# A fused decoder layer on one Trainium2 core: expert weights in 4 MB halves, the block tables moved behind block 9, the residual added on TensorE

## The chip, the cores and the metric

The kernel runs on one core of a Trainium2 chip. The metric is the device time of one execution in microseconds (us). TensorE is PE in the profile (its weight loads are PEld), VectorE is DVE, ScalarE is ACT, GpSimd is POOL, SyncE is SP; a q behind an engine's name is its sequencer. All data is float32.

## The reference

One layer on 256 tokens of width 1024: a projection, a gated delta network and a dilated attention, an output projection, and a mixture of experts. Only the last is touched here:

```python
h = x + concat(a, b) @ W_out
logits = rmsnorm(h) @ w_router + b_router            # 32 experts
top_v, top_e = top_k(logits, 4); gates = softmax(top_v)
for each expert e and its tokens x:
    gu = x @ w_gu[e] + b_gu[e]                       # 1024 -> 2048
    g, u = min(gu[:, :1024], 7), clip(gu[:, 1024:], -7, 7)
    y = ((u + 1) * g * sigmoid(1.702 * g)) @ w_dn[e] + b_dn[e]
    out[token] += gate * y
return h + out
```

## The kernel before

The first fifth of the time is the layer up to the router. The mixture then runs as blocks of at most 64 slots of one expert. Blocks 0 to 31 are experts 0 to 31 in order; further blocks exist only where an expert has over 64 tokens, and with this input there are exactly 32. Each block reads 12 MB of weights: gate and up as four tiles of 2 MB (two of eight row groups k each), down as two of 2 MB. Gate and up have two sets of buffers in SBUF, down has one.

PE, for one block (`gate_up`, L1550, then `combine`, L1519, and `rest`, L1582): four matmuls of the bias (L1560); for each k four matmuls over 512 columns (L1569, two records each); `combine`, which adds the former block's result, scaled by the gates, to PSUM banks 0 to 3 (L1523); two transposes of the gates (L1586); the gather of the next block's tokens (L1317); the transposes of the activation (L1593), which wait for the chain of four DVE operations L1105, L1106, L1109, L1115; the transposes of the gathered rows (L1509); and the down matmuls (L1606). A wait in PE's order holds all that is behind it. The semaphores `wgu_used` (one count per tile of gate/up) and `wdn_used` (per tile of down) tell SP that a buffer is free.

SP issues the loads in an order written out by hand (`load_block(m, ahead)`, L414): the four tiles of gate/up of block m + 1 and the two of down of block m, each behind the wait for its buffer. For blocks 1 to 6 down comes last, for 7 to 9 it moves forward, from 10 on it comes first. Before the first of these loads SP waits for the table of experts (`tab_ready`, L407) and loads it into registers.

The tables (which expert a block has, each token's slot in it, its gate) are made at the start of block 0, in pieces between the k: `block_table` (L1529) after k = 0, `slot_tables` (L1536) after k = 3, and `open_mixture` (L1269), which puts the gated b_down into banks 0 to 3, after k = 5. DVE makes the counts and limits (L1047 to L1087), ACT copies the transposes (L720, L660). After the last block `combine` runs once more, DVE adds the residual in four steps (L1126) and SP writes four pieces out (L445).

## Time and profile before

| | us |
|---|---|
| median of 3 runs (1151.19 to 1152.13) | 1151.99 |
| the profiled execution | 1153.8 |
| its span, first to last instruction | 1152.0 |
| PE busy in the span | 1106.2 (96%) |
| DVE, ACT, POOL busy | 276.8, 153.8, 8.0 |
| matmuls L1569 (gate/up), 2048 records | 453.8 |
| matmuls L1606 (down), 1024 records | 226.8 |
| HBM read, over the span | 424.29 MB, 371 GB/s |
| share of the last chain: DMA, PE | 51%, 45% |

A PE that is busy for 96% need not be at its peak: matmuls are pipelined, and a record lasts longer (595 ns) than the distance to the next. The time of a stretch of PE is therefore read from the start of one group to the start of the next. A block's length is the distance between two L1560.

### The profile page before, as it was taken

What the parts mean: (1) busy time and instruction counts of PE and PEld (TensorE: products, weight loads), DVE (VectorE), ACT (ScalarE), POOL (GpSimd) and SP (SyncE); (2) the same over time, 40 slices, a digit from 0 to 9 for tenths busy, and PEclk for the clock granted to TensorE, in tenths of its full rate; (3) what the DMA queues carried; (4) which work ended last, traced back from release to release, by engine and by line L of the source; (5) the groups of instructions that cost most, each with busy time, mean ns of one, the idle gap of its engine ahead of it and who ended that gap; (6) DMA issues with size and microseconds to landing.
All of it is one profiled execution on the core that took longest, in us unless ns stands there. A gap on an engine that the chain in (4) does not pass through costs nothing.

```text
span 1152.0 us, 13668 instructions
## 1 busy us (share of the span) xinstructions
PE 1106.2 (96%) x5240; PEld 445.3 (39%) x5240; DVE 276.8 (24%) x624; ACT 153.8 (13%) x284; POOL 8.0 (1%) x28
## 2 busy tenths in 40 slices
PE   9999989999999999999999999999999999999997
PEld 7855755533333333333333333333333333333332
DVE  3642344331111111111111111111111111111112
ACT  3521314410000000000000000000000000000000
POOL 1000000000000000000000000000000000000000
PEclk9999998999999999999999999999999999999999
DMA  9594110989999999999999999999999999999995
GB/s 326 99 351 160 73 74 10 374 352 389 427 428 428 428 429 428 428 388 431 430 428 428 428 428 429 428 428 429 428 429 429 428 430 429 428 428 428 428 428 240
DMA packets 42648, 427.20 MB, mean 371 GB/s; under 512 B 6755, under 2 KB 8900, under 8 KB 18052
## 3 DMA queue, kind: packets, MB, share of 16 engines
q1 hardware_dynamic: 40340, 426.86, 89.1%
q10 hardware_dynamic: 2288, 0.07, 0.1%
q8 instruction: 13, 0.21, 0.1%
q14 instruction: 7, 0.06, 0.0%
HBM read 424.29 MB, written 2.62 MB: 371 GB/s over the span
## 4 chain that ended last, share of the span: by engine, by line
DMA 51%; PE 45%; DVE 2%; ACT 1%; issue 1%; SPq 1%; DVEq 0%; ACTq 0%
DMA store<-in_w_gate_up_dram 50%; PE bank L1569 14%; PE bank L1606 7%; PE bank L1194 5%; PE bank L1201 4%; PE bank L1393 4%; PE bank L1265 3%; PE bank L1317 2%; PE bank L1523 2%; PE bank L1560 1%; DMA store<-in_w_in_dram 1%; PE bank L1509 1%; ACT conv L731 1%; PE bank L1586 0%; PE bank L1297 0%
## 5 line engine op out<-in xcount | busy, mean ns | idle before, releaser
L1569 PE MATMUL bank<-store,conv 128*64 128x512 f32 x2048 | 453.8, 595 | 21.1 <-DMA store<-in_w_gate_up_dram 21.0
L1569 PEld LDWEIGHTS bank<-store,conv 128*64 128x64 f32 x2048 | 141.2, 137 | 329.9 <-issue 280.5
L1606 PE MATMUL bank<-store,conv 128*64 128x512 f32 x1024 | 226.8, 595 | 0.3 <-DVE conv L1118 0.3
L1105 DVE TENSOR_SCALAR conv<-bank 128x512 f32<-128x512 f32 x32 | 22.1, 691 | 661.9 <-PE bank L1569 661.9
L1606 PEld LDWEIGHTS bank<-store,conv 128*64 128x64 f32 x1024 | 70.6, 137 | 132.4 <-issue 128.0
L727 ACT ACTIVATE conv<-conv 128x512 f32<-128x512 f32 x32 | 20.1, 630 | 505.8 <-DVE conv L1105 505.8
L1523 PE MATMUL bank<-qkT 64*128 64x512 f32 x256 | 63.6, 615 | 0.7 <-ACT qkT L733 0.7
L1317 PE MATMUL bank<-arena,qkT 128*64 128x512 f32 x264 | 64.2, 605 | 0.0
L1194 PE MATMUL bank<-store 128*128 128x512 f32 x128 | 58.1, 607 | 0.0
L733 ACT COPY qkT<-bank 128x512 f32<-128x512 f32 x32 | 18.7, 585 | 252.9 <-PE bank L1606 252.9
L1201 PE MATMUL bank<-store 128*128 128x256 f32 x192 | 42.7, 380 | 0.9 <-DMA store<-in_w_in_dram 0.9
L1201 PEld LDWEIGHTS bank<-store 128*128 128x128 f32 x192 | 36.2, 190 | 7.2 <-issue 2.5
L1523 PEld LDWEIGHTS bank<-qkT 64*128 64x128 f32 x256 | 22.0, 186 | 41.8 <-issue 40.2
L1194 PEld LDWEIGHTS bank<-store 128*128 128x128 f32 x128 | 24.3, 195 | 27.5 <-issue 27.4
L1560 PE MATMUL bank<-store,qkT 32*64 32x512 f32 x256 | 34.8, 613 | 0.0
L1115 DVE TENSOR_TENSOR conv<-conv 128x512 f32<-128x512 f32 x32 | 34.4, 1076 | 0.0
L1118 DVE COPY conv<-bank 128x512 f32<-128x512 f32 x32 | 22.1, 691 | 50.5 <-PE bank L1593 50.5
L1265 PE MATMUL bank<-store,conv 128*128 128x512 f32 x64 | 30.8, 626 | 0.4 <-DVE conv L1032 0.4
L1393 PE MATMUL bank<-store 128*128 128x128 f32 x200 | 27.0, 290 | 1.9 <-DVE arena L957 1.6
L1509 PE MATMUL bank<-ident,conv 128*128 128x128 f32 x132 | 24.6, 309 | 3.5 <-ACT conv L718 0.4
L1393 PEld LDWEIGHTS bank<-store 128*128 128x128 f32 x200 | 25.5, 203 | 5.1 <-issue 2.4
L1317 PEld LDWEIGHTS bank<-arena,qkT 128*64 128x64 f32 x264 | 15.9, 136 | 24.0 <-issue 24.0
(282 smaller groups left out, 567.5 us busy)
## 6 DMA issues: line engine op xcount, KB each, us to landing
store<-in_w_gate_up_dram SPq DMA_DIRECT2D x128, 2048.0 KB, 26.8
store<-in_w_down_dram SPq DMA_DIRECT2D x64, 2048.0 KB, 19.4
store<-in_w_in_dram SPq DMA_DIRECT2D x7, 2048.0 KB, 23.1
store<-in_w_out_dram SPq DMA_DIRECT2D x1, 4096.0 KB, 18.0
bias_by_distance<-store SPq DMA_DIRECT2D x1, 1536.0 KB
hx<-in_x_dram SPq DMA_DIRECT2D x2, 512.0 KB, 3.9
store<-bias_by_distance SPq DMA_DIRECT2D x1, 1024.0 KB, 8.2
out_dram<-hx SPq DMA_DIRECT2D x4, 256.0 KB, 2.2
```

What stands on the lines that cost most here:

```text
L1105: dve.tensor_scalar(gt, bank[4][:], LIMIT, None, ALU.min).then_inc(g_min, 1)
L1115: dve.tensor_tensor(gt.rearrange("q (c r) -> q r c", c=4), up.rearrange("q (r c) -> q r c", c=4), sg.rearrange("q (r c) -> q r c", c=4), A ...
L1194: ins = mm(dst[:], xnT[:, k, half * P:(half + 1) * P], w[:, k, :], start=k == 0, stop=k == KT - 1)
L1201: ins = mm(dst[:, c * S:(c + 1) * S], w[:, k, c0:c0 + P], xnT[:, k, :], start=k == 0, stop=k == KT - 1)
L1265: last = mm(bank[H_BANK[i]][:], lhsT[:, t * P:(t + 1) * P], wout[:, k, hf * 512:(hf + 1) * 512], start=k == HG, stop=k == HG - 1)
L1317: ins = mm(bank[6][SLOTS * hf:SLOTS * (hf + 1), :], SEL[:, t, :], hn[:, t, hf * 512:(hf + 1) * 512], start=t == 0, stop=t == T - 1)
L1393: last = mm(dst[:, c], lhsT(h) if callable(lhsT) else lhsT[:, c], rhs(h) if callable(rhs) else rhs[:, c], start=start, stop=stop)
L1509: last = tp(bank[6][:, c * P:(c + 1) * P], xg_rows[:, c], ident[:])
L1523: last = mm(bank[2 * t + hf][:], SGT[SLOTS * hf:SLOTS * (hf + 1), t * P:(t + 1) * P], yb[SLOTS * hf:SLOTS * (hf + 1), :], start=False, sto ...
L1560: mm(dst[SLOTS * hf:SLOTS * (hf + 1), :], oh_cur[N_EXP * c:N_EXP * (c + 1), :], bgu[N_EXP * c:N_EXP * (c + 1), :], start=True, stop=False)
L1569: last = mm(dst[SLOTS * hf:SLOTS * (hf + 1), :], xgT[:, c:c + SLOTS], store[:, slot_at(k, odd) + c0:slot_at(k, odd) + c0 + 512], start=Fal ...
L1606: last = mm(bank[7][SLOTS * hf:SLOTS * (hf + 1), :], actT[:, c:c + SLOTS], w[:, hf * 512:(hf + 1) * 512], start=f == 0, stop=f == KT - 1)
```

## The change

- Expert numbers of blocks 1 to 28 are the loop's own count. SP no longer waits for a table before the loads; it does so before the load of block 30's gate/up (`tab_ready` 4).
- Gate/up of blocks 2 to 9 and of the last block come in tiles of 2 MB as before; those of blocks 10 to 30 come as two halves of 4 MB, whose rows in HBM are 32 KB in one piece for each partition (the tiles have 16 KB). SP waits until both tiles of a half are used, and PE waits for the whole half, before k = 0 and k = 4.
- Down of block m is issued behind gate/up of block m + 1 up to m = 15, between the halves at 16, and ahead of them from 17 on.
- Blocks 0 to 9 read slot numbers and gates directly from what the router leaves. The counts, tables and b_down stand in one piece (`late_tables`, `add_mixture`) on PE between blocks 9 and 10. There the residual is added too, as four matmuls with the identity. DVE and ACT do their part after their own block 9; PE waits for `tab_ready` 7 and then reads two registers. The rest of DVE's list of table operations is unchanged but for one more, and its copies are of 16 columns in place of 48.
- In blocks 10 to 30 `combine` stands after k = 3, in the middle of gate/up. In the last block it stands after k = 5 with the transposes of the gates, and the gather for a next block is left out.
- The out pieces are copied from PSUM, two by DVE (written out by SP) and two by ACT (which issues their DMAs itself).
- The two loads of b_down (64 KB each) stand behind those of b_gate_up on SP. The matmuls of the counts and one transpose leave PE's part ahead of block 0.

```diff
-EARLY_BLOCKS = 6
+FINE_BLOCKS = 10
+LATE_BLOCKS = 16
...
+            src = w_gate_up[0][e_ap, half * 4 * P:(half + 1) * 4 * P, :]
+            return src.rearrange("a (p i) n -> p (a i n)", p=P)
...
-            sp.wait_ge(tab_ready, 3)
...
+            def load_block(m, e, e_next, down_at, whole, off=0):
+                odd = sp.value_load(parity[0:1, bass.ds(m + (off + 1), 1)], min_val=0, max_val=1)
+                for half in range(2):
+                    if half == down_at:
+                        load_down(m, e, off)
+                    if whole:
+                        sp.wait_ge(wgu_used, 4 * m + (4 * off + 2 * half - 2))
+                        sp.wait_ge(ld_tile[2 * half], 16 * m + (16 * off + 16))
+                        sp.dma_start(half_dst(half, odd), expert_half(bass.ds(e_next, 1), half)
+                                     ).then_inc(ld_tile[2 * half], 16)
+                        continue
+                    for i in (2 * half, 2 * half + 1):
+                        sp.wait_ge(wgu_used, 4 * m + (4 * off + i - 3))
+                        if i % 2 == 0:
+                            sp.wait_ge(ld_tile[i], 16 * m + (16 * off + 16))
                         sp.dma_start(tile_dst(i, odd), expert_tile(bass.ds(e_next, 1), i)).then_inc(ld_tile[i], 16)
+                if down_at == 2:
+                    load_down(m, e, off)
...
-            with sp.Fori(1, EARLY_BLOCKS + 1) as b:
-                load_block(b, 4)
-            for k in (3, 2, 1):
-                load_block(EARLY_BLOCKS + 4 - k, k)
-            with sp.Fori(EARLY_BLOCKS + 4, n_blocks - 1) as b:
-                load_block(b, 0)
...
+            with sp.Fori(1, FINE_BLOCKS - 1) as b:
+                load_block(b, b, b + 1, 2, False)
+            with sp.Fori(FINE_BLOCKS - 1, LATE_BLOCKS) as b:
+                load_block(b, b, b + 1, 2, True)
+            with sp.Fori(LATE_BLOCKS, LATE_BLOCKS + 1) as b:
+                load_block(b, b, b + 1, 1, True)
+            with sp.Fori(LATE_BLOCKS + 1, N_EXP - 3) as b:
+                load_block(b, b, b + 1, 0, True)
...
+            load_block(three_less, expert_of(three_less + 1), e_last, 0, False, off=1)
...
+                act.wait_ge(acc_done, 2 * t + 2)
+                act.copy(hx[:, t, 512:D], bank[2 * t + 1][:]).then_inc(out_right, 1)
+                act.wait_ge(out_right, t + 1)
+                act.dma_start(out[0, t * P:(t + 1) * P, 512:D], hx[:, t, 512:D]).then_inc(st_right, 16)
...
+            for t in range(T):
+                dve.wait_ge(acc_done, 2 * t + 1)
+                dve.tensor_copy(hx[:, t, 0:512], bank[2 * t][:]).then_inc(out_left, 1)
...
+            def add_mixture(t):
                 pe.wait_ge(gT_ready, t + 1)
                 for hf in range(2):
-                    rows = slice(N_EXP * hf, N_EXP * (hf + 1))
-                    mm(bank[2 * t + hf][:], gT[t][rows, :], bdn[rows, :], start=True, stop=False,
+                    rows = slice(2 * N_EXP + N_EXP * hf, 3 * N_EXP + N_EXP * hf)
+                    mm(bank[2 * t + hf][:], gT[t][rows, :], bdn[rows, :], start=False, stop=False,
                        skip_group_check=True)
+                    mm(bank[2 * t + hf][:], ident[:], hx[:, t, 512 * hf:512 * (hf + 1)], start=False, stop=False,
...
+            def late_tables():
+                for i in range(T):
+                    ins = mm(bank[4][0:N_EXP, 0:1], mask[i], ones[:, 0:1], start=i == 0, stop=i == T - 1)
+                Tally(pe, cnt_psum).mark(ins)
+                pe.wait_ge(gates_ready, T)
+                for t in range(T):
+                    ins = tp(bank[5][:, t * P:(t + 1) * P], gates4[t], ident[:])
+                Tally(pe, gT_psum).mark(ins)
+                for t in range(T):
+                    ins = tp(bank[5][0:N_EXP, S + t * P:S + (t + 1) * P], rm[t], ident[:])
+                Tally(pe, rt_psum).mark(ins)
+                pe.wait_ge(nb_ready, 1)
+                mm(bank[4][0:N_EXP, 1:2], ucum[0:N_EXP, 0:N_EXP], more, start=True, stop=True)
+                mm(bank[4][0:N_EXP, 2:3], ustr[0:N_EXP, 0:N_EXP], more, start=True, stop=True)
+                Tally(pe, end_psum).mark(mm(bank[4][0:1, 4:5], ones[0:N_EXP, 0:1], more, start=True, stop=True))
+                for t in range(T):
+                    add_mixture(t)
...
+                pe.wait_ge(tab_ready, 3)
...
+                pe.wait_ge(tab_ready, 7)
...
+                    if k % 4 == 0:
                         pe.wait_ge(ld_tile[k // 2], 16 * (b + 1))
+                    elif k % 4 == 2 and not whole:
+                        pe.wait_ge(ld_tile[k // 2], 16 * (FINE_BLOCKS + 1) if last else 16 * (b + 1))
...
+                    if k == (5 if last else 3) and (whole or last):
+                        pe.wait_ge(y_ready, b)
+                        combine()
+                        if last:
+                            turn_gates(b)
...
+                if not last:
+                    turn_gates(b)
+                    pe.wait_ge(S_ready, b + T + 1)
+                    gather(0)
+                    gather(1).then_inc(xg_psum, 1)
...
+            def whole_block(b, odd):
+                gate_up(b, odd, whole=True)
+                rest(b)
+            def last_block(b, odd):
+                gate_up(b, odd, last=True)
+                rest(b, last=True)
...
+            expert_block(1, 1)
+            with pe.Fori(1, FINE_BLOCKS // 2) as pair:
+                expert_block(2 * pair, 0)
+                expert_block(2 * pair + 1, 1)
+            late_tables()
...
-            with pe.Fori(0, (two_less + 1) >> 1) as pair:
-                expert_block(2 * pair + 1, 1)
-                expert_block(2 * pair + 2, 0)
+            with pe.Fori(FINE_BLOCKS // 2, (two_less + 1) >> 1) as pair:
+                whole_block(2 * pair, 0)
+                whole_block(2 * pair + 1, 1)
             with pe.If((two_less + 1) & 1):
-                expert_block(two_less + 1, 1)
+                whole_block(two_less, 0)
+                last_block(two_less + 1, 1)
+            with pe.Else():
+                last_block(two_less + 1, 0)
```

## Rows read from the trace of the kernel before

**Rows 1.** The page: granted clock and GB/s in 40 slices of 28.8 us

```profile
PEclk9999998999999999999999999999999999999999
GB/s 326 99 351 160 73 74 10 374 352 389 427 428 428 428 429 428 428 388 431 430 428 428 428 428 429 428 428 429 428 429 429 428 430 429 428 428 428 428 428 240
```

**Rows 2.** The chain that ended last, in time: start us, us, what

```profile
193.16 3.44 PE bank L1265 x8
...
264.28 1.02 PE bank L1560 x8
265.30 13.88 PE bank L1569 x64
279.18 1.92 PE bank L1523 x8
...
284.77 7.02 PE bank L1606 x32
291.79 1.02 PE bank L1560 x8
...
542.65 28.06 DMA store<-in_w_gate_up_dram
```

**Rows 3.** Timeline of the SP queue, DMA issues: start us, us, line, what

```profile
238.83 14.29 SPq L428 DMA_DIRECT2D store<-in_w_gate_up_dram  x4
261.04 4.22 SPq L423 DMA_DIRECT2D store<-in_w_down_dram  x2
...
701.26 3.79 SPq L423 DMA_DIRECT2D store<-in_w_down_dram  x2
...
730.59 3.78 SPq L423 DMA_DIRECT2D store<-in_w_down_dram  x2
```

**Rows 4.** Windows: us, PE, PEld, DVE, ACT, POOL busy (x count), PEclk, DMA share, GB/s

```profile
600.00:659.00 59.00, 58.80 (x280) 19.84 (x278) 10.81 (x22) 4.34 (x8) 0.00 (x0) 1.00 1.01 428
```

**Rows 5.** Timeline of block 31 and the end, PE and SP queue

```profile
1115.53 1.09 PE L1560 MATMUL bank<-store,qkT 32*64 32x512 f32 x8
...
1128.70 3.65 PE L1569 MATMUL bank<-store,conv 128*64 128x512 f32 x16 [1.24 <-DMA store<-in_w_gate_up_dram]
...
1137.88 7.09 PE L1606 MATMUL bank<-store,conv 128*64 128x512 f32 x32
...
1147.53 2.12 SPq L445 DMA_DIRECT2D out_dram<-hx  x4
```

**Rows 6.** Timeline of block 0 on PE: start us, us, line, shapes, [idle before]

```profile
232.24 1.09 PE L1560 MATMUL bank<-store,qkT 32*64 32x512 f32 x8
...
235.62 5.37 PE L1569 MATMUL bank<-store,conv 128*64 128x512 f32 x24
240.92 0.33 PE L1538 MATMUL bank<-ident,qkT 128*128 128x128 f32 x1
...
243.41 3.65 PE L1569 MATMUL bank<-store,conv 128*64 128x512 f32 x16
246.99 1.99 PE L1273 MATMUL bank<-qkT,conv 32*128 32x512 f32 x8
248.91 3.65 PE L1569 MATMUL bank<-store,conv 128*64 128x512 f32 x16
252.49 0.44 PE L1586 MATMUL bank<-ident,qkT 128*128 128x128 f32 x2
...
255.75 0.66 PE L1593 MATMUL bank<-ident,conv 128*128 128x128 f32 x4 [0.95 <-DVE conv L1115]
...
257.19 7.09 PE L1606 MATMUL bank<-store,conv 128*64 128x512 f32 x32 [0.30 <-DVE conv L1118]
```

**Rows 7.** Timeline of DVE, its first instruction after the tables

```profile
245.31 0.42 DVE L1094 TENSOR_SCALAR qkT<-slot,qkT 128x64 f32<-128x64 f32 x2 [1.26 <-issue]
```

**Rows 8.** Windows with the columns of rows 4, around a drop of the clock

```profile
81.00:84.80 3.80, 1.48 (x14) 1.27 (x12) 2.07 (x3) 0.20 (x1) 1.04 (x1) 1.00 1.05 388
85.00:88.40 3.40, 3.40 (x5) 1.33 (x4) 2.55 (x4) 0.00 (x0) 0.00 (x0) 0.50 1.10 425
```

More of the change, by code:

```diff
@@ L386, in _ @@
             sp.dma_start(wr, w_router[0].rearrange("(k p) e -> p k e", p=P)).then_inc(ld_wr, 16)
-            for c in range(2):
-                sp.dma_start(bdn[N_EXP * c:N_EXP * (c + 1), :], b_down[0][:, c * 512:(c + 1) * 512]).then_inc(ld_moe, 16)
             sp.wait_ge(o_psum, 6)
@@ L395, in _ @@
                              ).then_inc(ld_moe, 16)
+            for c in range(2):
+                rows = slice(2 * N_EXP + N_EXP * c, 3 * N_EXP + N_EXP * c)
+                sp.dma_start(bdn[rows, :], b_down[0][:, c * 512:(c + 1) * 512]).then_inc(ld_moe, 16)
             sp.wait_ge(s_max, 6)
@@ L1118, in _ @@
                 dve.tensor_copy(actT, bank[4][:]).then_inc(actT_ready, 1)
-                dve.wait_ge(xgT_psum, b + 2)
-                turned_rows().then_inc(xgT_ready, 1)
-            for i in range(2 * T):
-                t, hf = divmod(i, 2)
-                dve.wait_ge(acc_done, i + 1)
-                v = hx[:, t, hf * 512:(hf + 1) * 512]
-                dve.tensor_tensor(v, bank[i][:], v, ALU.add).then_inc(out_ready, 1)
+                if not last:
+                    dve.wait_ge(xgT_psum, b + 2)
+                    turned_rows().then_inc(xgT_ready, 1)
@@ new lines, in _ @@
+            dve.wait_ge(dve_step, st.n)
+            with dve.Fori(0, FINE_BLOCKS) as b:
+                expert_block(b)
+            g4 = Tally(dve, gates_ready)
+            for t in range(T):
+                g4.mark(dve.tensor_copy(gates4[t].rearrange("p (c e) -> p c e", c=4),
+                                        gates[t].unsqueeze(1).to_broadcast([P, 4, N_EXP])))
+            nb = Tally(dve, nb_ready)
+            dve.wait_ge(cnt_psum, 1)
+            cnt = bank[4][0:N_EXP, 0:1]
+            st.step(dve.tensor_scalar(more, cnt, float(SLOTS), None, ALU.is_gt))
@@ new lines, in _ @@
+            for j in range(2, S // SLOTS):
+                ins = dve.scalar_tensor_tensor(out=more, in0=cnt, scalar=float(j * SLOTS), in1=more,
+                                               op0=ALU.is_gt, op1=ALU.add)
+                (st.step if j < S // SLOTS - 1 else nb.mark)(ins)
+            dve.wait_ge(end_psum, 1)
+            tr = Tally(dve, tab_ready)
+            st.step(dve.tensor_scalar(col[0:N_EXP, 25:27], bank[4][0:N_EXP, 1:3], float(N_EXP), None, ALU.add))
+            st.step(dve.tensor_scalar(oh, iota_b[:], beg, None, ALU.is_ge))
@@ new lines, in _ @@
+            st.step(dve.scalar_tensor_tensor(out=oh, in0=iota_b[:], scalar=end, in1=oh, op0=ALU.is_lt,
+                                             op1=ALU.mult))
+            st.step(dve.tensor_scalar(since, iota_b[:], beg, 1.0, ALU.subtract, ALU.add))
+            tr.mark(dve.tensor_scalar(nbl[0:1, MAXB:MAXB + 1], bank[4][0:1, 4:5], float(N_EXP), None, ALU.add))
+            rt = Tally(dve, rt_ready)
+            st.step(dve.scalar_tensor_tensor(out=ohr, in0=since, scalar=-float(SLOTS), in1=oh, op0=ALU.mult,
+                                             op1=ALU.mult))
@@ new lines, in _ @@
+            rt.mark(dve.tensor_tensor(oh, oh, own[:], ALU.add))
+            for less in (2, 3):
+                tr.mark(dve.tensor_scalar(nbl[0:1, MAXB + less - 1:MAXB + less], bank[4][0:1, 4:5], float(N_EXP - less),
+                                          None, ALU.add))
+            dve.wait_ge(nbl_psum, 1)
+            tr.mark(dve.tensor_copy(nbl[0:1, 0:MAXB], bank[4][0:1, 128:128 + MAXB]))
+            dve.wait_ge(tab_psum, 1)
+            more_b = slice(N_EXP, MAXB)
+            tr.mark(dve.tensor_copy(RM[:, :, more_b], bank[5][:, 0:T * MAXB].rearrange(
+                "p (t b) -> p t b", t=T)[:, :, more_b]))
@@ new lines, in _ @@
+            tr.mark(dve.tensor_copy(oh4[:, more_b], bank[5][:, 256 + N_EXP:256 + MAXB]))
+            tr.step(dve.tensor_copy(GB[:, :, more_b], bank[5][:, 128:128 + T * MAXB].rearrange(
+                "p (t b) -> p t b", t=T)[:, :, more_b]))
+            two_less = dve.value_load(nbl[0:1, MAXB + 1:MAXB + 2], min_val=N_EXP - 2, max_val=NB_MAX - 2)
+            with dve.Fori(FINE_BLOCKS, two_less + 1) as b:
+                expert_block(b)
+            expert_block(two_less + 1, last=True)
+            for t in range(T):
+                dve.wait_ge(acc_done, 2 * t + 1)
+                dve.tensor_copy(hx[:, t, 0:512], bank[2 * t][:]).then_inc(out_left, 1)
@@ L1552, in gate_up @@
+            def gate_up(b, odd, whole=False, last=False):
+                first = isinstance(b, int) and b == 0
                 if first:
```

239 lines of the change are left out of this document (90 added, 149 removed).

## The prediction, made before the changed kernel was run

> **What bounds the kernel now.** I read the page's slices first [rows 1]. From the ninth slice on (230 us) DMA moves 428 GB/s almost without a break; three slices fall short, with 352, 389 and 388 GB/s. The page has PE busy for 96% of the span. So two resources run close together, and the question is which one ends each block. The chain of waits in time [rows 2] gives PE for blocks 1 to 10, with one period: L1560 starts at 264.28 and at 291.79, 27.51 us apart. After 542.65 it names DMA, but that label alone is not enough: it merges loads that merely follow each other. The SP queue's timeline decides [rows 3]. Its down loads are released by PE's own progress. From 261.04 to 701.26 there are 16 block lengths, so 27.51 us each: PE alone sets the pace up to block 17, however full the queue looks. From 701.26 to 730.59 it is 29.33, and block 31 starts at 1115.53 [rows 5], 14 periods of 29.36 behind block 17 (704.5). There DMA rules: 12.58 MB at 428 GB/s [rows 4] are 29.37 us, and PE waits 1.24 us for the last tile even in block 31 [rows 5].
>
> What matters for the change: PE alone, at 27.51 for 30 blocks from 264.28, would start block 31 at 1089.6. It starts at 1115.5. **PE has 26 us to spare**, and no more. Work put on PE is free up to that sum, and costs in full beyond it.
>
> **The change on DMA.** The first load now needs no table. Before, it was issued at 238.83 [rows 3]; tile 0 of block 0 is used by 232.24 + 1.02 + 3.5 = 236.8, so I take 236.5, 2.3 us earlier. The short slices [rows 1] are 76, 39 and 40 GB/s below 428, which is 5.1, 2.6 and 2.7 us of queue without work: the first two at the start, the third at block 10, where down moves ahead. Some 2 us remain while the queue starts again. So DMA could deliver the last gate/up tile 8.5 us earlier, at about 1120 in place of 1128.7.
>
> For the 4 MB halves the trace has no row. The nearest is the mix of strided gate/up tiles and contiguous down tiles, which runs at one steady 428 GB/s [rows 4]: the queue hides what a single DMA costs. I take no difference. The bounds are 0.5% to either side of DMA's 29.37 per block, 0.15 us, 3 us over 21 blocks, and none of it shows while PE sets the pace. The Trainium skill, "DMA: Bandwidth & Descriptors", section Bandwidth, gives 341 GB/s for single transfers of 1 MB and 425 for 16 MB. By that rule a 4 MB half would be a few per cent quicker than two tiles, some 20 us of DMA over 21 blocks as an estimate; the trace does not agree for queued tiles, which have 428 at 2 MB, and the sum stays the one below either way, because it is PE's.
>
> Edits that I cost at nothing: the two b_down loads stand ahead of two of block 1's tiles, for which PE has until 258; without that cover they would hold SP for two issues, some 1 us. SP's register loads per block fall under its waits. The moved reads of the router's result on DVE (blocks 0 to 9) have the same shapes.
>
> **The change on PE, step by step.**
> 1. Ahead of block 0 a transpose and small matmuls go: 0.25 us (a quarter of L1593's 0.66 [rows 6] and some 0.1). Block 0 starts at 232.0.
> 2. Block 0 took 264.28 - 232.24 = 32.04 [rows 2, 6]. Without tables it is 1.02 (L1560) + 13.88 (L1569 unbroken [rows 2]) + 4.70 (from 252.49, the end of gate/up, to the down matmuls at 257.19 [rows 6]) + 7.02 (L1606 [rows 2]) = 26.6, and 0.2 for the first tile's wait on DVE. It ends at 258.8, 5.5 us earlier. This is the gain.
> 3. Blocks 1 to 9 keep 27.51: 506.4. Down now comes last in the queue up to block 15. In block 1 it is the sixth load of 4.9 us (29.37 / 6) behind a start of the queue at some 238.5, so it has landed by 268, and PE needs its second half at 258.8 + 24: 14 us to spare, and 29.37 - 27.51 = 1.86 less in each block, so block 9 waits some 0.5: 506.9.
> 4. `late_tables` on PE's path, nothing covers it. (a) Counts, four transposes (0.66 [rows 6]), three small matmuls and a trip to DVE and back between them: 1.4, bounds 1.0 and 2.5 (all of block 0's table stretch, 243.41 - 240.92 [rows 6]). (b) `add_mixture`: b_down 1.92 (246.99 to 248.91 [rows 6]), the identity four times a pair of k at 128 x 128 like L1265, 3.44 for four [rows 2]: 5.4 in all. ACT's copies and DVE's limits are hidden under it. (c) Block 0's eight table matmuls: 2.49 less a transpose and a wait of 0.5, plus the one for the numbers, 2.0. (d) DVE's three copies 0.6, then PE reads two registers. DVE idled for 1.26 for one such read and a loop's start [rows 7]; two make 1.8. In block 0 the sequencer read ahead under the matmuls, now the wait stands before it. Sum 11.2, bounds 9.5 and 14.
> 5. The clock. At 81 to 84.8 PE was busy for 1.48 of 3.8 us, and the granted clock was 0.50 (1.2 GHz) for the 3.4 us that followed [rows 8]. Part (c) and (d) look like this. Half speed for 3.4 us loses 1.7. I take it; bounds 0 and 3.4. The Trainium skill, "TensorE: Matmul & The Clock Gate", Part 1, says that the throttled state is the default and that activity releases it, which speaks against any idle stretch put between blocks. By that rule the 1.7 are due, without it the sum ends at 1156.5; rows 8 agree with the rule. Block 10 starts at 506.9 + 11.2 + 1.7 = 519.8.
> 6. Blocks 10 to 30. `combine` (1.92 [rows 2]) filled PE while DVE ran its chain; from the end of gate/up to the down matmuls it was 284.77 - 279.18 = 5.59 [rows 2]. Without `combine` there PE waits for DVE: block 0 shows 4.70, with 0.95 idle [rows 6]. So only 0.89 of the 1.92 is saved. The loop of L1569 is cut in two runs of 32 records, 7.01 each (L1606 has 7.02 for 32 [rows 2]). A block becomes 1.02 + 14.02 + 1.92 + 4.70 + 7.02 = 28.68, which is **1.17 more than 27.51**. In a PE that waits for DMA this would be free. 21 blocks: 602.3, to 1122.1.
> 7. Block 31: 1.02 + 14.2 (three runs) + 1.92 + 0.37 + 4.70 + 7.02 = 29.2, to 1151.3. Before, the down matmuls ended at 1137.88 + 7.02 = 1144.9 [rows 5].
> 8. The end. From 1144.9 to the end of the span were 7.1 us, with the last DMA issued at about 1149.3 [rows 5]. Two engines copy in turn, but ACT issues a DMA between its two copies: 6.9, bounds 6 and 8.
>
> Sum: 1151.3 + 6.9 = 1158.2 for the span, against 1152.0. The profiled execution lasted 1153.8, which is 1.8 above the median of the runs; with the same 6.2 added I expect 1160.0 in a profile and **1158 as the median**, 0.5% slower.
>
> Does DMA keep out of it? At block 17 down moves ahead and waits for down of block 16 to be used. PE is then 16 us behind its old timetable (719.8 + against 704.5), so the queue runs empty for some 9 us. Its halves land about 9 us before PE needs them, and lose 29.37 - 28.68 = 0.7 per block; after 13 blocks nothing or a small wait (up to 2 us) is left. The last gate/up tile lands at about 1129; PE wants it at 1135.
>
> **Rivals.**
> - DMA still ends every block, so that the halves and the moved `combine` are free. Then the last tile at 1120, 3.6 for its matmuls, 4.70, 7.02 and 6.9 give 1142, 0.9% faster. It decides if PE's added work stays below its 26 us: my steps 4 to 7 add 12.9 + 24.6 + 0.5 and take 5.8, so 32. To come out over 0.2% faster the sum must lose 8.5: a block of 28.3 in place of 28.68, or `late_tables` with its clock at 4.4, where its matmuls alone are over 8. For it: the queue is full in the trace. Against it: step 6 is read from block 0, which has just this order.
> - Nothing to be measured. A measurement of this kernel tells 0.2%, 2.3 us, from no change. No clock drop (-1.7), `late_tables` at 9.5 (-1.7), breaks of L1569 free (-1.5): 1153.3.
> - Worse: the half clock for 6.8 us (+1.7), tables at 13 (+1.8), DMA late in the last blocks after the hole at 17 (+2): 1163.7.
>
> **How the numbers follow.** Forecast (1154.3 to 1161.5) 0.53; worse 0.17; nothing 0.17; faster 0.13. The 80% range leaves out the faster half of the fast case and a tail above: 1148 to 1165. Faster by over 0.2%: 0.13, within: 0.17, slower: 0.70.
>
> **What the new profile would show.** The distance from bias matmul to bias matmul (L1560 before): 27.5 up to 9, then 28.7, never 29.4. Block 1 at 258.8, block 10 at about 520, block 31 at 1122. A slice near 500 to 530 where PE is below 9 tenths, with a clock drop; a slice of low GB/s near 700 to 720 (block 17), with PE's only idle time behind gate/up, on DVE's product (L1115 before). The first gate/up load at 236.5. I am wrong if PE waits for half loads from block 18 on, or if the distance from the table's first to block 10's first matmul is under 8 us.

## The result, and the profile after

The changed kernel takes 1166.32 us (median of 4 runs, 1164.87 to 1166.66) against 1152.06 for the kernel before in the same session (4 runs, 1151.19 to 1153.31). The ratio is 1.0121, 95% interval 1.0103 to 1.0138: 14 us slower. I had forecast 1158, with 1148 to 1165 as the range. The direction came out, and so did the bound that moved from DMA to PE; the size did not, and the largest single error was the price of `add_mixture` (step 4 below). The profiled execution lasted 1166.64, its span 1164.8.

First the page: granted clock and GB/s in 40 slices of 29.1 us, and the shares of the chain that ended last.

```profile
PEclk9999999999999999999999999999999999999999
...
GB/s 326 97 383 119 73 73 5 397 416 428 426 429 428 429 429 427 432 430 388 419 432 431 430 362 291 433 429 430 431 430 431 431 430 431 431 430 430 432 428 145
...
PE 84%; DVE 7%; DMA 5%; issue 3%; ACT 1%; SPq 0%; DVEq 0%; ACTq 0%
```

Before, DMA had 51% of that chain, and from 290 us on the queue ran full but for one slice of 388 [rows 1]. Now DMA has 5%. Two slices (362 and 291) show a queue without work, 388 and 419 a shorter gap. The bound has moved to PE. Where PE's time went is read from its timeline. First one block of the late stretch, block 19 (start us, us, line, shapes, count, [idle before]):

```profile
782.78 1.09 PE L1617 MATMUL bank<-store,qkT 32*64 32x512 f32 x8
783.79 7.09 PE L1629 MATMUL bank<-store,conv 128*64 128x512 f32 x32
790.81 1.99 PE L1569 MATMUL bank<-qkT 64*128 64x512 f32 x8
792.73 7.09 PE L1629 MATMUL bank<-store,conv 128*64 128x512 f32 x32
799.75 0.44 PE L1643 MATMUL bank<-ident,qkT 128*128 128x128 f32 x2
...
803.01 0.66 PE L1655 MATMUL bank<-ident,conv 128*128 128x128 f32 x4 [0.96 <-DVE conv L1125]
...
804.45 7.09 PE L1669 MATMUL bank<-store,conv 128*64 128x512 f32 x32 [0.30 <-DVE conv L1128]
811.47 1.09 PE L1617 MATMUL bank<-store,qkT 32*64 32x512 f32 x8
```

The block is 811.47 - 782.78 = 28.69 us, where PE had 27.51 [rows 2]. `combine` (L1569 here) stands between the halves, and behind gate/up PE now waits 0.96 us for DVE, as block 0 did before [rows 6]. Nothing in it waits for DMA. All the blocks from 11 to 30 are alike.

Then the stretch between blocks 9 and 10:

```profile
499.47 3.65 PE L1669 MATMUL bank<-store,conv 128*64 128x512 f32 x16 [0.27 <-DMA store<-in_w_down_dram]
504.27 3.65 PE L1669 MATMUL bank<-store,conv 128*64 128x512 f32 x16 [1.15 <-DMA store<-in_w_down_dram]
507.85 0.29 PE L1578 MATMUL bank<-ones,qkT 128*32 128x1 f32 x4
...
509.13 1.12 PE L1330 MATMUL bank<-store,conv 32*128 32x512 f32 x2
510.18 1.13 PE L1332 MATMUL bank<-hx,ident 128*128 128x512 f32 x2
...
517.56 0.24 PE L1595 MATMUL bank<-store,col 32*1 32x48 f32 x2
...
519.11 0.38 PE L1603 MATMUL bank<-store,rep 32*128 32x48 f32 x2
521.89 1.98 PE L1617 MATMUL bank<-store,qkT 32*64 32x512 f32 x8 [2.40 <-issue]
```

Block 9 waits twice for down weights. `late_tables` runs from 507.85 to 521.89, 14.04 us, of which `add_mixture` has 509.13 to 517.56, 8.43: each b_down call (L1330) and each residual call (L1332) takes 1.05, from its start to the next one's. Last, the clock around it and in the last block (window, busy us and count of PE, PEld, DVE, ACT, POOL, then the granted clock, the share of DMA and GB/s), and the last block itself:

```profile
517.20:520.60 3.40, 2.29 (x18) 1.71 (x16) 0.57 (x4) 0.00 (x0) 0.00 (x0) 1.00 0.94 405
520.70:527.40 6.70, 5.51 (x18) 1.47 (x20) 0.94 (x4) 0.00 (x0) 0.00 (x0) 0.50 0.97 413
1144.50:1148.60 4.10, 0.66 (x4) 0.42 (x4) 3.19 (x5) 0.89 (x2) 0.00 (x0) 1.00 0.00 0
1148.70:1152.00 3.30, 2.83 (x8) 0.98 (x10) 0.42 (x1) 0.00 (x0) 0.00 (x0) 0.50 0.02 5
```

```profile
1127.04 1.09 PE L1617 MATMUL bank<-store,qkT 32*64 32x512 f32 x8
...
1140.80 3.65 PE L1629 MATMUL bank<-store,conv 128*64 128x512 f32 x16
1147.73 0.66 PE L1655 MATMUL bank<-ident,conv 128*128 128x128 f32 x4 [3.28 <-DVE conv L1125]
1149.17 8.51 PE L1669 MATMUL bank<-store,conv 128*64 128x512 f32 x32 [0.78 <-DVE conv L1128]
```

Twice PE idles, is granted half its clock (1.2 GHz in place of 2.4), and works slowly just where it has work again. Once these are the first matmuls of block 10, behind the tables: the block takes 31.37 in place of 28.69. The other time it is the down matmuls of the last block, 8.51 in place of 7.09.

### The profile page after: what moved, and what is told of

It is laid out like the page before. It is cut to its first block, busy times and chain, and to the rows that moved or that the text cites. A ratio compares the mean times of both kernels' runs of the same rounds, so it can differ in the third digit from the quotient of the medians.

```text
span 1164.8 us, 13191 instructions
## 1 busy us (share of the span) xinstructions
PE 1106.0 (95%) x5236; PEld 446.8 (38%) x5236; DVE 269.5 (23%) x621; ACT 151.8 (13%) x285; POOL 8.0 (1%) x28
## 4 chain that ended last, share of the span: by engine, by line
PE 84%; DVE 7%; DMA 5%; issue 3%; ACT 1%; SPq 0%; DVEq 0%; ACTq 0%
PE bank L1629 36%; PE bank L1669 19%; PE bank L1569 5%; PE bank L1250 5%; DMA store<-in_w_down_dram 4%; PE bank L1257 4%; PE bank L1443 3%; PE bank L1617 3%; PE bank L1321 2%; DVE conv L1125 2%; DVE conv L1128 1%; DVE conv L1115 1%; PE bank L1655 1%; PE bank L1372 1%; DMA store<-in_w_in_dram 1%
## 5 line engine op out<-in xcount | busy, mean ns | idle before, releaser
L1569 PE MATMUL bank<-qkT 64*128 64x512 f32 x256 | 63.6, 615 | 0.7 <-ACT qkT L755 0.7
L1655 PE MATMUL bank<-ident,conv 128*128 128x128 f32 x128 | 21.0, 287 | 24.3 <-DVE conv L1125 24.3
L1569 PEld LDWEIGHTS bank<-qkT 64*128 64x128 f32 x256 | 22.1, 186 | 41.8 <-issue 40.2
L1617 PE MATMUL bank<-store,qkT 32*64 32x512 f32 x256 | 35.7, 627 | 2.4 <-issue 2.4
L1250 PEld LDWEIGHTS bank<-store 128*128 128x128 f32 x128 | 24.2, 194 | 26.9 <-issue 26.8
L1655 PEld LDWEIGHTS bank<-ident,conv 128*128 128x128 f32 x128 | 13.4, 140 | 51.8 <-DVE conv L1125 44.5
L1321 PE MATMUL bank<-store,conv 128*128 128x512 f32 x64 | 29.1, 598 | 0.4 <-DVE conv L1071 0.4
```

The source lines that it names most:

```text
L1250: ins = mm(dst[:], xnT[:, k, half * P:(half + 1) * P], w[:, k, :], start=k == 0, stop=k == KT - 1)
L1321: last = mm(bank[H_BANK[i]][:], lhsT[:, t * P:(t + 1) * P], wout[:, k, hf * 512:(hf + 1) * 512], start=k == HG, stop=k == HG - 1)
L1569: last = mm(bank[2 * t + hf][:], SGT[SLOTS * hf:SLOTS * (hf + 1), t * P:(t + 1) * P], yb[SLOTS * hf:SLOTS * (hf + 1), :], start=first, sto ...
L1617: mm(dst[SLOTS * hf:SLOTS * (hf + 1), :], oh_cur[N_EXP * c:N_EXP * (c + 1), :], bgu[N_EXP * c:N_EXP * (c + 1), :], start=True, stop=False)
L1655: ins = tp(bank[4][:, c * P:(c + 1) * P], gt[:, c * P:(c + 1) * P], ident[:])
```

## The experiments

The ratios below are to the kernel before, measured in the same session. A number of us given as more or less is a difference of two such ratios, times 1152; the intervals of the ratios are 1 to 2 us to either side, so small differences rest on the rows of the profiles more than on the times. All kernels compute the whole result. "Block 31 from block 0" is the distance of their first bias matmuls (L1560 before, L1617 after). It leaves out the part ahead of block 0, which differed from profile to profile: 230.7 to 232.2 in five profiles of the kernel before and its variants, 230.2 to 231.2 in eleven of the changed one and its variants. The distance is 883.3 before and 896.4 after.

### combine back behind gate/up

```diff
-                    if k == (5 if last else 3) and (whole or last):
+                    if k == 5 and last:
...
                 gate_up(b, odd, whole=True)
+                pe.wait_ge(y_ready, b)
+                combine()
                 rest(b)
```

> combine goes back behind gate/up in blocks 10 to 30, where DVE's chain hides it; the rest is the changed kernel. My theory (PE sets the pace, and the place of combine costs 1.17 us in each of 21 blocks): bias matmuls 27.5 us apart from block 10 on, until the queue of weights is caught up with at about block 23; then 29.1 apart, by DMA. Block 31 starts at about 1114 in place of 1127, the span ends at about 1149, the median is about 1150, a ratio of 0.986 to the changed kernel. Rival (the cost of a block is the wait for 4 MB halves, and combine is free where it stands): blocks stay 28.7 apart and the time stays within 1 us of 1166.

Measured: 1154.35, ratio 1.0022 (1.0012 to 1.0032), 11 us less than the change. PE's blocks are 27.51 from 11 to 21, and 29.21 to 29.23 from 23 on. GB/s, and block 24, of which the second half is waited for:

```profile
GB/s 326 99 372 138 73 74 5 402 386 427 429 428 429 428 429 427 435 429 388 434 428 427 435 424 340 433 431 430 431 430 432 430 430 431 430 431 431 430 428 176
```

```profile
910.77 1.09 PE L1617 MATMUL bank<-store,qkT 32*64 32x512 f32 x8
911.78 7.09 PE L1629 MATMUL bank<-store,conv 128*64 128x512 f32 x32
920.37 7.09 PE L1629 MATMUL bank<-store,conv 128*64 128x512 f32 x32 [1.50 <-DMA store<-in_w_gate_up_dram]
```

So the 1.17 us per block are the place of `combine`, and are most of the loss. Yet the time missed my 1150 by 4. Block 31 is 884.9 from block 0, no earlier than before, though DMA starts sooner and takes 29.21 per block in place of 29.37. The row of GB/s says where the time went: the queue is short of work at 388 (2.8 us of a 28.8 us slice) and at 424 and 340 (6.4 us together).

### Pairs in add_mixture

```diff
                     mm(... gT[t][rows, :], bdn[rows, :] ...)
+                for hf in range(2):
                     mm(... ident[:], hx[:, t, 512 * hf:512 * (hf + 1)] ...)
```

> In add_mixture both b_down matmuls of a token tile are issued, then both residual ones, in place of one and one by turns; same work. My theory (a b_down matmul fills 32 rows of the array and two of them on different rows run side by side, unless a full matmul stands between them): the four b_down calls fall from 1.05 us to about 0.5 each, add_mixture from 8.4 us to about 6, the distance from the counts to block 10 from 14.0 to about 11.5, the median by 2 to 3 us, to 1163.6. Rival (each call costs 1.05 us for its own reasons, weight load or bank): add_mixture stays at 8.4 and the median at 1166.

Measured: 1163.57, ratio 1.0097 (1.0082 to 1.0112), 2.8 us less. The interval touches that of the change (1.0103 to 1.0138); the rows are clear:

```profile
509.16 1.13 PE L1330 MATMUL bank<-store,conv 32*128 32x512 f32 x4
510.21 1.98 PE L1333 MATMUL bank<-hx,ident 128*128 128x512 f32 x4
512.13 1.13 PE L1330 MATMUL bank<-store,conv 32*128 32x512 f32 x4
513.19 1.98 PE L1333 MATMUL bank<-hx,ident 128*128 128x512 f32 x4
515.10 0.24 PE L1596 MATMUL bank<-store,col 32*1 32x48 f32 x2
```

Two b_down calls (x4 records) now take the 1.05 us that one took. The residual calls fell too, from 1.05 to 0.96 each (1.92 for two). `add_mixture` is 515.10 - 509.16 = 5.94 in place of 8.43. The Trainium skill, "TensorE: Matmul & The Clock Gate", Part 3, says that matmuls on different 32-row strips of the array run at the same time; the trace agrees for neighbours, and shows that with a matmul on all 128 rows between them nothing of it is left.

### Matmuls on constants at the end of late_tables

```diff
                 Tally(pe, tab_psum).mark(ins)
+                pe.wait_ge(y_ready, FINE_BLOCKS)
+                filler(1)
                 pe.wait_ge(tab_ready, 7)
+                filler(3)
```

> Four matmuls on constants, whose result is overwritten, are issued around PE's wait and its register reads at the end of late_tables, so that PE idles less; the rest is the changed kernel. My theory (PE's half clock for 6.8 us from 520.6 follows from the idle stretch before it, and costs block 10 2.7 us): the clock stays full behind the tables, block 10 lasts 28.7 in place of 31.4, and the median falls by about 2.7 us less what the fillers delay (under 0.5): 1163.8. Rival (the drop comes whatever PE does there): block 10 stays at 31.4 and the median stays at 1166 or rises by the fillers' 0.5.

`filler(n)` is n matmuls of `ones` on `ones` over 256 columns, into a bank where nothing that is still needed stands.

Measured: 1163.38, ratio 1.0095 (1.0080 to 1.0111), 3.0 us less.

```profile
518.39 0.38 PE L1607 MATMUL bank<-store,rep 32*128 32x48 f32 x2
518.70 2.09 PE L1577 MATMUL bank<-ones 128*128 128x256 f32 x8
521.09 1.09 PE L1624 MATMUL bank<-store,qkT 32*64 32x512 f32 x8 [0.29 <-issue]
522.11 7.09 PE L1636 MATMUL bank<-store,conv 128*64 128x512 f32 x32
```

PE's hole of 2.40 us is filled, the distance from block 9 to block 10 stays (43.19 against 43.25), the clock stays full, and block 10 is 28.69 in place of 31.37. The drop is not chance: seven profiles without these matmuls have it, and none of the four with them (this one and three below).

### Gate/up in 2 MB tiles

```diff
-                load_block(b, b, b + 1, 2, True)
+                load_block(b, b, b + 1, 2, False)
...
-                    elif k % 4 == 2 and not whole:
+                    elif k % 4 == 2:
```

> Gate/up weights come as four 2 MB tiles in all blocks, as in the first kernel; PE waits for a tile in each quarter. My theory (the halves change neither PE's work nor the bytes per second by over 0.5%): the bias matmuls stay 28.7 apart, block 31 starts within 1.5 us of 1127, the median is 1166 +- 1.5. Landings of a block in steady state 0.15 us further apart (29.37 in place of 29.22), hidden. Rival (the halves are quicker by some per cent, as single transfers of more bytes would be): without them DMA falls behind PE from about block 20 on and the time rises by over 5 us. Second rival (the halves make PE wait, since it has to have 4 MB where it had 2): the time falls by over 3 us.

Measured: 1167.18, ratio 1.0126 (1.0111 to 1.0142), which is not to be told from the change's. The two windows of 600 to 659 us, of the change and then of this kernel (columns as above):

```profile
600.00:659.00 59.00, 56.09 (x266) 18.47 (x262) 11.95 (x26) 5.12 (x11) 0.00 (x0) 1.00 1.00 431
```

```profile
600.00:659.00 59.00, 55.52 (x268) 18.95 (x267) 11.27 (x23) 4.71 (x9) 0.00 (x0) 1.00 1.01 428
```

431 against 428 GB/s, 0.7%. The rule of the Trainium skill on single transfers ("DMA: Bandwidth & Descriptors", section Bandwidth), which the prediction cited, would have made it a few per cent. Beside it, this profile was granted half the clock for 3.4 us behind the tables in place of 6.8, and its block 10 took 30.33 in place of 31.37. The edit did not do that: a run below, which is the same as the change up to its last block, also had the 3.4 us, and 30.25. So the length of the drop differs from one execution to the next.

The halves have a price of their own, which I had overlooked:

```profile
GB/s 328 97 380 121 73 73 5 394 411 430 427 428 430 426 430 428 428 428 428 426 429 429 429 350 294 428 428 429 430 427 430 427 429 430 428 429 428 429 429 152
```

With tiles the slices behind the tables (524 to 582 us) are 428 and 426, where the change has 388 and 419, though the tables are as long; with halves and the shorter half clock they are 406 and 419. With halves SP waits until 4 MB are used before it loads again, and in that stretch the queue runs out of work.

### Down weights of blocks 7 to 9 between the halves

```diff
-            with sp.Fori(1, FINE_BLOCKS - 1) as b:
-                load_block(b, b, b + 1, 2, False)
+            with sp.Fori(1, FINE_BLOCKS - 3) as b:
+                load_block(b, b, b + 1, 2, False)
+            with sp.Fori(FINE_BLOCKS - 3, FINE_BLOCKS - 1) as b:
+                load_block(b, b, b + 1, 1, False)
...
```

> The changed kernel with the down weights of blocks 7 to 9 loaded between the halves of gate/up (as the kernel before did around block 8) in place of behind them. My theory (down weights come last in the queue, the queue started 1.5 us later against PE than I had reckoned, so blocks 8 and 9 wait 1.2 and 1.7 us for them): both waits go, blocks 8 and 9 are back at 27.5 and the median falls by 2.5 to 3 us, to 1163.5. Rival (DMA is behind as a whole, whatever the order): the waits move to gate/up of block 10 or stay, and the median stays within 0.7 of 1166.

Measured: 1163.83, ratio 1.0101 (1.0084 to 1.0118), 2.3 us less, an interval that overlaps the change's. Block 8 is back at 27.51, and blocks 9 and 10 start 1.2 and 3.0 us earlier from block 0 on.

### The three together

The edits are those of the three runs on `add_mixture`, on the end of `late_tables` and on the order of down; `combine` stays where the change has it.

> The changed kernel with the three small remedies together: pairs in add_mixture (2.7 us less alone), matmuls on constants at the end of late_tables (2.9 less alone), down weights of blocks 7 to 9 between the halves (2.5 less alone); combine stays inside gate/up. My theory (PE's path sets the end, so the three terms that I had too small simply add): 1166.3 - 2.7 - 2.9 - 2.5 = 1158.2, what I had forecast for the change, and blocks from 10 on 28.7 apart. Rival (they overlap, or DMA comes to the fore once PE is quicker): 1161 or more.

Measured: 1159.16, ratio 1.0063 (1.0049 to 1.0077). Block 31 is 888.2 from block 0, 8.1 less than in the change, the full sum. The last block gave back 0.9: there the half clock lasted 6.8 us in this profile, and 3.4 in the change's. So the three small terms are real and add. That the time lands within 1 us of my 1158.2 is partly luck: the forecast had 1.7 for a half clock behind the tables and 0.5 for waits, which this kernel doesn't have, and nothing for the one in the last block, which it does.

### Matmuls on constants in the last block

```diff
-                if not last:
+                if last:
+                    for _ in range(4):
+                        mm(bank[6][:, 0:S], ones[:], ...)
+                else:
                     turn_gates(b)
```

> The changed kernel with four matmuls on constants behind gate/up of the last block, where PE idles for 3.3 us waiting for DVE; nothing else. My theory (that idle stretch lowers the clock at 1148.7, so the last 32 down matmuls take 8.5 in place of 7.0): they take 7.0 to 7.2, the span ends 1.3 us earlier, the median is 1165.0. Rival (the clock falls anyway, or falls a little later and costs the same): 1166.3. Within the two the medians alone may not tell; the row of the down matmuls does.

Measured: 1164.42, ratio 1.0116 (1.0100 to 1.0132). The median alone tells nothing, since the interval overlaps the change's; the rows do:

```profile
1142.31 1.99 PE L1650 MATMUL bank<-ones 128*128 128x256 f32 x8
1145.65 0.66 PE L1658 MATMUL bank<-ident,conv 128*128 128x128 f32 x4 [1.35 <-DVE conv L1125]
1147.09 7.09 PE L1672 MATMUL bank<-store,conv 128*64 128x512 f32 x32 [0.78 <-DVE conv L1128]
```

7.09 in place of 8.51. The block takes 29.2 from its bias matmuls (1124.97) to the end of the down matmuls, the length that I had forecast. All eight profiles with `combine` and the gates inside the last block's gate/up and no such matmuls had a drop there, of 3.4 or 6.8 us.

### What PE can lose for nothing: combine moved alone

The kernel before, with `combine` behind the fourth pair of k in blocks 11 to 30:

```diff
+                    if mid and k == 3:
+                        pe.wait_ge(y_ready, b)
+                        combine()
```

> The kernel before, with combine moved into gate/up (behind the fourth pair of k) in blocks 11 to 30 and nothing else of the change. My theory (PE alone had 26 us to spare behind DMA, and each moved combine takes 1.17 us of it): 20 blocks cost 23.4 us, which fits under the 26: blocks that PE paces are 28.7 apart, the later ones stay 29.4 apart by DMA, block 31 starts within 1 us of 1115.5, the median is 1152 (within 2 us). Rival (a block costs its 1.17 wherever it stands, DMA being no bound): 1175. So the move of combine alone would be nearly free, and only together with the late tables does it cost.

Measured: 1153.02, ratio 1.0011 (1.0001 to 1.0021). The blocks are 28.69 up to 26 and then 29.36; block 31 is 883.1 from block 0, against 883.3. 20 x 1.17 = 23 us of PE cost about 1 us. Spread out, the 26 us to spare were there. In the change the same move, in 21 blocks, costs 11 us (the first experiment). There the late tables (14.0), the half clock (2.7) and the waits (2.9), less the 5.4 won in block 0, had taken 14 of the 26 ahead of it. By the sum 12 are left for 24.8 us, and 13 are paid; block 31 tells 11.5.

### The same in one lump

The kernel before with 23 (then 40) matmuls on constants between blocks 10 and 11, and then with the 23 between blocks 18 and 19:

```diff
+            for _ in range(23):
+                mm(bank[5][:], ones[:], ...)
```

> The kernel before, with 23 matmuls on constants put between blocks 10 and 11 (some 0.86 us each, 20 us of PE), result overwritten. My theory (26 us to spare on PE): the time stays within 1.5 us of 1152. Rival (PE's path sets the end throughout): 1172.

> The kernel before, with 40 of the same matmuls at the same place, 34 us of PE. My theory (26 us to spare, less up to 1 for a queue of weights that runs empty for a while behind block 17): 8 to 11 us slower than the kernel before, 1160 to 1163. Rival (all of it counts): 1186; rival (none): 1152.

> The kernel before, with the same 23 matmuls on constants (20 us of PE) as in the run that cost 17 us, but between blocks 18 and 19 in place of 10 and 11. My theory (a lump costs what it makes the queue of weights idle; at block 10 the queue is still nearly as far ahead as the buffers let it, at block 18 it has lost 1.86 us per block and can use the lump to catch up): the queue idles for some 4 us, PE is free of DMA for 8 blocks behind it, the time rises by about 4 us, to 1156. Rival (a lump of PE work costs its length wherever it stands): 1169. Rival (it is free, as my 26 us to spare would have it): 1152.

Measured behind block 10: 1169.41, ratio 1.0148 (1.0130 to 1.0167), and 1183.49, ratio 1.0270 (1.0253 to 1.0287). Both of my expectations fell: 20 us cost 17, 34 us cost 31. Behind block 18 the same 20 us cost 7.6: 1159.36, ratio 1.0066 (1.0052 to 1.0080), over 3 more than expected, but neither 0 nor 20. GB/s of the three, in that order:

```profile
GB/s 327 106 391 99 72 73 16 412 319 424 425 430 430 427 427 430 428 388 431 207 412 430 429 429 426 430 429 427 428 430 429 427 428 429 429 428 428 430 428 240
```

```profile
GB/s 325 97 386 104 71 72 50 394 336 426 429 429 427 430 429 427 430 391 430 100 310 429 428 428 429 428 429 429 428 429 428 428 430 427 428 430 428 428 429 240
```

```profile
GB/s 326 97 372 138 73 73 10 376 360 407 427 430 427 429 429 428 428 390 430 428 429 427 429 430 428 427 429 358 431 428 427 431 428 428 427 431 428 428 427 229
```

The first misses (428 - 207) / 428 of a 29.2 us slice and (428 - 412) / 428 of the next: 16.2 us of idle queue. Its block 31 starts 16.4 later from block 0 on than before. The second (slices of 29.6 us) misses 22.7 + 8.2 = 30.9, and is 31.0 later. The third misses 4.7, and is 5.5 later; its median is 7.6 up, and the 2 us between stay open. **A lump costs what it makes the queue idle**, not its excess over PE's reserve. The reading that fits is this: up to block 10 DMA is nearly as far ahead as the buffers let it be, so when the blocks stop, it soon stops too. By block 18 it has lost its lead, and the lump lets it win it back: behind it PE ran 27.51 for 7 blocks before it waited again.

### combine back, and down ahead of gate/up four blocks later

```diff
-LATE_BLOCKS = 16
+LATE_BLOCKS = 19
...
-            with sp.Fori(LATE_BLOCKS, LATE_BLOCKS + 1) as b:
+            with sp.Fori(LATE_BLOCKS, LATE_BLOCKS + 2) as b:
```

> The changed kernel with combine back behind gate/up, as in the run with that alone (1154.35), and the down weights put ahead of gate/up from block 21 on in place of block 17 (between the halves in 19 and 20). My theory (with combine back, DMA ends every block from 23 on, so only its idle time counts, and it idles some 7 us at block 17, where down has to wait for PE to use the former): the hole in GB/s at 660 to 720 us goes, DMA comes to pace PE later, the time falls by 6 to 7 us to about 1147.7, faster than the kernel before by 0.4%. The 14 us of the late tables then cost nothing at the end. Rival (a hole opens anyway wherever down changes place): 1153 to 1155.

Measured: 1150.89, ratio 0.9992 (0.9982 to 1.0003): 3.5 less than with `combine` back alone, not 6 to 7.

```profile
GB/s 323 101 368 146 73 74 5 380 391 427 427 428 428 428 428 428 437 427 383 436 434 423 436 431 427 435 425 434 407 433 431 430 429 433 431 430 430 432 428 158
```

The hole at 660 to 720 us is gone. What I had overlooked is the 383: in the slice of the late tables the queue idles for 3.1 us, so they do cost something at the end. Another 1.5 are at 407. The tables are not the only cause of the 383, as the run in 2 MB tiles has no such gap with tables of the same length: lump and halves make it together.

### All of it: faster than both

`combine` back, down between the halves in 7 to 9 and the later switch of the last kernel, the pairs, and constants in both holes; each edit is shown above.

> As the last, with the three small remedies of late_tables and blocks 7 to 9 added, and four matmuls on constants in the last block, where PE idles for 3.3 us and the clock falls. My theory (DMA paces PE from some block on, so 8 us less of PE's work ahead of it are worth nothing; only the last block, behind the last load, can gain): 1146 to 1147.5, block 31 starts at the same time as in the last within 0.7 us. Rival (PE's path sets the end): 8 us less than the last, 1140.

Measured: **1145.89, ratio 0.9948 (0.9934 to 0.9963)**, the fastest of all.

```profile
GB/s 326 101 367 149 74 74 5 350 414 428 425 429 429 429 427 429 430 435 429 428 433 427 434 427 434 427 433 429 418 432 431 430 431 430 431 431 431 431 425 198
```

In place of 383 stands 429. Block 31 is 877.1 from block 0, 3.7 less than in the last kernel, where I had expected 0.7 at most: by the slices it is those 3.1 us of idle queue. Which of the edits ahead of block 11 removed them is not told by this run; each of the three alone, with `combine` in its new place, has 419 to 424 in that slice, where two profiles without them have 388 and 406. The last block gave some 2.

### And in tiles

The same kernel with the edit of the run in 2 MB tiles.

> As the last, with gate/up in 2 MB tiles throughout. My theory (a 4 MB half saves 0.04 us per 2 MB, 0.15 us per block, seen in the distances that DMA sets, 29.21 against 29.36): 21 blocks cost 3.2 us, 1149.5 to 1150.5; the late blocks are 29.36 apart. Rival (halves and tiles are worth the same in time): within 0.7 us of the last.

Measured: 1148.51, ratio 0.9970 (0.9961 to 0.9979), 2.5 more. The number fits my theory, but the rows don't. First of the kernel with halves, then of that with tiles, block 30, in the latter the wait of block 31, and the last down matmuls:

```profile
1087.72 7.09 PE L1641 MATMUL bank<-store,conv 128*64 128x512 f32 x32 [1.48 <-DMA store<-in_w_gate_up_dram]
...
1129.48 7.09 PE L1683 MATMUL bank<-store,conv 128*64 128x512 f32 x32 [0.78 <-DVE conv L1132]
```

```profile
1091.68 3.65 PE L1641 MATMUL bank<-store,conv 128*64 128x512 f32 x16 [1.24 <-DMA store<-in_w_gate_up_dram]
...
1116.58 3.65 PE L1641 MATMUL bank<-store,conv 128*64 128x512 f32 x16 [0.59 <-DMA store<-in_w_gate_up_dram]
...
1130.82 8.69 PE L1683 MATMUL bank<-store,conv 128*64 128x512 f32 x32 [0.79 <-DVE conv L1132]
```

Block 31 is 877.3 from block 0 with tiles, 877.1 with halves. DMA delivered the halves of block 30 4.0 us earlier (the waits end at 1087.72 and 1091.68), but a half has 7.02 us of matmuls behind its last byte and a tile 3.5, so nearly all that DMA gained PE had to give back. The difference at the end is a wait of 0.59 and, for the greater part, a half clock in the last block (8.69 against 7.09), which the constants did not prevent this time. Yet chance does not explain the medians: all 12 times with tiles (1147.22 to 1149.89) lie above all 5 with halves (1144.74 to 1146.11). Whether the drop in the last block comes with the tiles, and what else the halves are worth, stays open.

## Why the prediction was wrong in size, step by step

The step that failed most is 4(b), `add_mixture`, priced from matmuls with other neighbours: 5.4 forecast, 8.43 measured. The waits of step 3 (0.5, measured 2.9) and the clock of steps 5 and 7 make up the rest. The spans add up: forecast 1158.2, measured 1164.8, 6.6 apart.

| step | forecast | measured | error |
|---|---|---|---|
| 1, block 0 starts | 232.0 | 230.68 | -1.3 |
| 2, block 0 | 26.8 | 26.62 | -0.2 |
| 3, waits in blocks 1 to 9 | 0.5 | 2.9 | +2.4 |
| 4, late_tables | 11.2 | 14.04 | +2.8 |
| 5, clock | 1.7 | 2.68 | +1.0 |
| 6, blocks 10 to 30 | 602.3 | 602.5 | +0.2 |
| 7, block 31 | 29.2 | 30.6 | +1.4 |
| 8, end | 6.9 | 7.2 | +0.3 |

- **What bounds the kernel** and **step 6**, the heart of it, were right: PE takes over, and a block is 28.69 where I had 28.68. That came from block 0 of the profile before, which had the same order of work. It alone adds 21 x 1.18 = 24.8 us to PE's path. The start of block 17 that the text works out from it (719.8) should have been 519.8 + 7 x 28.68 = 720.6; nothing hangs on it.
- **Step 4 failed in (b)**, `add_mixture`: 5.4 forecast, 8.43 measured. I took 1.92 for b_down from rows 6, where four calls follow one another on other rows of the array. In the change a residual matmul stands between every two, so each is paid alone: 4.2, which is 2.3 of the error. The other 0.8 is the residual, 3.44 forecast from L1265 and 4.2 measured. With the pairs restored it was 5.94 in all, close to the forecast. (a), (c) and (d) were 1.28, 1.8 and 2.55 against 1.4, 2.0 and 2.4.
- **Step 3 failed in the start of the queue.** I had the first load issued at 236.5, 4.5 behind the start of block 0; it was issued at 235.67, 5.0 behind. Block 9's down is the 54th load: counted from block 0's start the forecast has it landed at 238.5 + 54 x 4.895 - 232.0 = 270.8, and it landed at 504.27 - 230.68 = 273.6, 2.8 late. From 262 us on the slices are 426 to 432, so most of it should lie in the start; how it divides is not shown. Down stands last in the queue, so it was down that came late: the waits of blocks 8 and 9 are 1.2 and 1.7. The run with another order took them away. I had worked out the lead for block 1 (14 us to spare) and let it run down to block 9 with a remainder of 0.5, smaller than its error.
- **Steps 5 and 7** are the clock. Step 5 stayed within its bounds (0 to 3.4). In step 7 I had not looked for a drop at all, though rows 8 had the pattern, an idle PE and then half the clock, and my own step had PE wait for DVE with nothing left to fill the time: 3.28 us, then half clock. The run with constants there gives 29.2.
- **Step 1** is for the most part no gain of the change. The kernel before with an edit far behind it had block 0 at 230.69, 231.03, 232.06 and 232.18 in four profiles. The two late ones, like the profile that I worked from (232.24), were granted half the clock for 3.4 us at 211; the two early ones were not, and neither was the change. First the kernel before, then the change (columns as above):

```profile
211.30:214.70 3.40, 3.40 (x6) 1.33 (x5) 1.67 (x11) 2.79 (x4) 0.00 (x0) 0.50 0.97 401
211.30:214.70 3.40, 3.40 (x9) 1.52 (x8) 1.74 (x12) 2.93 (x4) 0.00 (x0) 1.00 0.96 398
```

The profile that I worked from was thus a late one, 1.7 above its median, that of the change 0.3 above. So of the 8.1 us by which the median exceeded my 1158.2, 6.6 are in the table and the rest is this. The 1.3 us that the table has in my favour here are luck of the two profiles, not of the forecast.
- **DMA**: first load at 235.67 for 236.5; halves 0.5 to 0.7% quicker than tiles, at the edge of my bounds; the hole at block 17 was forecast at 9 us and was 14 (362 and 291 in 29.1 us slices: 4.7 + 9.5), since PE was 21 us behind its old timetable and not 16. It cost nothing in the change, as PE was the bound.
- **"Work put on PE is free up to that sum"** was wrong as a rule. The sum of 26 holds only for work that is spread over the blocks. It did no harm to the forecast, since PE was beyond its reserve either way, but it misled three of my expectations (20 us and 34 us in a lump, and the late tables being free).
- **The rivals**: the case "worse", 1163.7, was nearest, and its three causes were the right kind (clock, tables, DMA), though the wait for DMA that it put into the last blocks came in blocks 8 and 9. DMA as the bound, 1142, would have needed `combine` where it was: with that, and a queue that idles for little more than 1 us behind 260 us, it came to 1145.9.

## What to carry to other kernels

Where two resources run close together, ask of added work not only whether the other has time to spare, but whether its queue stays full meanwhile: spread over blocks 23 us of PE cost 1, and 20 in one piece early cost 17. The slices of GB/s give how much later the last block starts to within a microsecond; the medians lay up to 3 us above that. Take a duration only from a row whose neighbours are the same as in the new place: here a full matmul between every two b_down calls doubled their price. And the two stretches in which PE idled, for 2.4 and 3.3 us, were paid twice, once as they stood and once in the clock behind them. A few matmuls on constants cost nothing there; behind the tables they returned 3 us, in the last block 1.4 by the rows of one profile, and in one of three they did not help.

## What was not expected of the hardware

- Two b_down calls of 32 rows took 1.05 us as neighbours, and one alone took 1.05 as well with a 128-row matmul on either side.
- With `combine` inside gate/up, the half clock behind the tables lasted 3.4 us in two profiles and 6.8 in three (block 10: 30.3 in both, or 31.0 to 31.4); constants kept the clock full in the last block in two profiles and not in a third.
- Where DMA sets the pace, blocks are 29.21 apart with 4 MB halves and 29.37 with 2 MB tiles, 0.5%, and in the pair of kernels above PE's coarser wait took nearly all of it back (block 31 at 877.1 and 877.3).
